# Expert stage of a two-layer hybrid block: padded groups of 32 rows on four 32-column tiles, and a third set of expert weights

## What is computed

```python
def moe(h, w_router, b_router, w1_l, w3_l, w2_l):
    comb = route(hf, w_router, b_router)          # top 2 of 4 experts in the best of 4 groups
    def chunk(args):
        xc, gc = args
        a = jnp.einsum('td,edf->tef', xc, w1_l)   # w1, w3: (16, 1024, 512)
        b = jnp.einsum('td,edf->tef', xc, w3_l)
        u = jax.nn.silu(a) * b * gc[..., None]
        return jnp.einsum('tef,efd->td', u, w2_l) # w2: (16, 512, 1024)
```

## Time and profile before

| what | value |
|---|---|
| median of the three runs | 1327.61 us |
| span of the profiled execution | 1325.8 us, 1.8 us less than the median |
| PE / PEld / DVE / ACT / POOL busy | 82% / 46% / 26% / 16% / 6% |
| bytes over the DMA engines | 328.6 MB, 248 GB/s on average |
| expert stage of layer 0, first up product to last down product | 428.7 to 733.75 us |
| expert stage of layer 1 | 1031.5 to 1296.4 us |
| granted TensorE clock, mean | 0.918 of 2.4 GHz |

### The profile page before, as it was taken

How to read it: one execution, slowest core, us unless ns; L and a number is a source line. 1 busy time by engine, 2 the same in 40 slices (tenths; PEclk the granted TensorE clock), 3 DMA queues, 4 the chain that set the end, 5 groups by cost and what they waited for, 6 DMA issues and landing times.

```text
span 1325.8 us, 18500 instructions
## 1 busy us (share of the span) xinstructions
PE 1081.6 (82%) x6246; PEld 604.7 (46%) x6247; DVE 345.4 (26%) x812; ACT 208.4 (16%) x487; POOL 79.0 (6%) x126
## 2 busy tenths in 40 slices
PE   2799989988981999999899189989892898788771
PEld 1446447765450544444346044647642454344430
DVE  2201147565342100101011430157624011000002
ACT  1110023432010111111101211023300111011001
POOL 2000000001002000000000300000101000000001
PEclk8899999989985999999999689999985799999896
DMA  9923116576135899999369671313645699999993
GB/s 330 374 91 127 64 70 238 202 258 226 43 131 208 319 396 395 398 397 384 122 227 397 214 269 64 127 64 128 240 158 198 234 332 397 396 396 397 397 397 110
DMA packets 142294, 328.60 MB, mean 248 GB/s; under 512 B 6552, under 2 KB 8760, under 8 KB 142240
## 3 DMA queue, kind: packets, MB, share of 16 engines
q1 hardware_dynamic: 125424, 287.84, 58.9%
q0 software_dynamic: 7856, 25.61, 5.4%
q10 hardware_dynamic: 8960, 14.40, 3.1%
HBM read 308.10 MB, written 19.73 MB: 247 GB/s over the span
## 4 chain that ended last, share of the span: by engine, by line
PE 56%; DMA 29%; DVE 7%; ACT 3%; issue 3%; POOL 2%; SPq 0%; ACTq 0%; DVEq 0%; POOLq 0%
DMA ring<-in_w 23%; PE S L1217 17%; PE S L1398 10%; PE S L1327 6%; PE O L1281 4%; PE T L1155 3%; PE AUX L1172 3%; DMA ring<-in_w_ada 3%; PE S L1432 2%; PE T L1432 2%; PE S L1248 2%; PE S L1402 2%; ACT R L643 1%; PE S L1437 1%; DVE R L916 1%
## 5 line engine op out<-in xcount | busy, mean ns | idle before, releaser
L1217 PE MATMUL S<-ring,hT 128*128 128x512 f32 (+1 forms) x576 | 226.0, 548 | 2.3 <-ACT hT L587 2.3
L1402 PE MATMUL S<-ring,R 128*64 128x256 f32 x1472 | 181.1, 405 | 33.0 <-DMA ring<-in_w 28.3
L1402 PEld LDWEIGHTS S<-ring,R 128*64 128x64 f32 x1472 | 114.5, 146 | 106.3 <-DMA ring<-in_w 40.3
L1217 PEld LDWEIGHTS S<-ring,hT 128*128 128x128 f32 x576 | 108.0, 191 | 104.3 <-issue 98.6
L1398 PE MATMUL S<-ring,R 128*128 128x512 f32 x320 | 144.1, 610 | 6.5 <-issue 3.3
L1155 PE MATMUL T<-cst,R 128*128 128x128 f32 (+1 forms) x497 | 80.1, 292 | 64.2 <-DVE R L793 30.4
L1088 DVE SCALAR_TENSOR_TENSOR R<-R,S 128x256 f32<-128x256 f32 (+1 forms) x33 | 16.6, 502 | 412.7 <-ACT R L694 412.7
L1155 PEld LDWEIGHTS T<-cst,R 128*128 128x128 f32 (+1 forms) x497 | 60.2, 151 | 93.4 <-DVE R L793 30.7
L1398 PEld LDWEIGHTS S<-ring,R 128*128 128x128 f32 x320 | 62.1, 195 | 87.2 <-issue 82.4
L1437 PE MATMUL S<-ring,R 128*64 128x512 f32 x368 | 84.0, 598 | 9.6 <-DMA ring<-in_w 5.7
L1327 PE MATMUL S<-ring,hT 128*128 128x512 f32 x192 | 85.6, 607 | 2.3 <-issue 2.3
(11 more groups left out here) (143 smaller groups left out, 756.8 us busy)
## 6 DMA issues: line engine op xcount, KB each, us to landing
ring<-in_w SPq DMA_DIRECT2D x96, 2048.0 KB, 11.5
ring<-in_w_ada SPq DMA_DIRECT2D x24, 2048.0 KB, 8.1
ring<-in_w_in SPq DMA_DIRECT2D x8, 2048.0 KB, 10.8
R<-x_d POOLq DMA_DIRECT2D x45, 256.0 KB, 5.7
ring<-in_w_out SPq DMA_DIRECT2D x4, 2048.0 KB, 9.8
R<-mod_d SPq DMA_DIRECT2D x12, 512.0 KB, 9.6
y_d<-R ACTq DMA_DIRECT2D x46, 128.0 KB, 5.3
y_d<-R ACTq DMA_DIRECT2D x20, 256.0 KB, 6.5
```

What stands on the lines that cost most here:

```text
L1217: ins = pe.matmul(S[:, i % 4, 0:width], hT[:, k, t * P:(t + 1) * P], w[:, k, :], start=(k == 0), stop=(k == KC - 1))
L1402: ins = pe.matmul(S[64 * h:64 * h + 64, i, 0:256], xT[:, half, k % 4, k // 4, 0:64], part[i][:, k, h * 256:h * 256 + 256], start=(k == 0), ...
```

## The change

Every expert's rows now start at a multiple of 32 rows in x_d and y_d, and an item is always one group of 32 rows. An expert with c rows has max(1, ceil(c/32)) groups. All of x_d, and the part of y_d that no group might write, are zeroed early in layer 0, with 30 DMAs of 128 rows each, 15.7 MB together. On TensorE the stationary operand is 128x32 and the four column tiles take a quarter of the output columns each (128 moving columns in the up products, 256 in the down product). The order in an item is: up with w1, the transposes of the next group's rows, the transpose of the last group's u, up with w3, the down product of the last group. xg, xT, u_s, uT, th, t2 and y_s have one buffer each. ACT issues four stores per item in place of two, and it copies the next y only when the four stores of the last one have landed. POOL fetches group i+1 only when group i has been transposed.

The weights have nine regions in place of six: hT and two parts of R2, which nothing uses in the expert stage, are the third set. SP issues the load of an expert when the expert three before it is done, still with at most two in flight. gF is therefore loaded at the end of the stage, into hT. The weights ka, va and kvb of layer 1's projection are issued ahead of the wait for the end of layer 0's experts. The order of some loads in layer 1's attention changes too, and the counts are ready ahead of the gates' computation in place of behind it.

The diff, cut to its core (inside the loops, waits on counts_ready and register steps are left out without a mark):

```diff
-TILE = 64
-MAXW = TOK // P
+ROWS = 32
+MAXG = TOK // ROWS
+SETS = 3
...
+    n_groups = [TOPK * TOK // ROWS + NE, TOPK * SEQ // ROWS + NE]
+    x_tiles = [-(-(g + 1) * ROWS // P) for g in n_groups]
...
-        xg = R2[:, 0:1536].rearrange("p (b n) -> p b n", b=3)
-        y_s = R2[:, 4096:6144].rearrange("p (b n) -> p b n", b=2)
+        zeros = R3[:, 4096:5120]
+        xg = R3[:, 0:256]
+        xT = R3[:, 256:512].rearrange("p (h j t) -> p h j t", h=4, j=2)
+        u_s, uT, th, t2 = R3[:, 512:640], R3[:, 640:768], R3[:, 768:896], R3[:, 896:1024]
+        y_s = R2[:, 9376:9632]
...
         def load_expert(l, e, part):
-            load(("e", l, e, part), 3 * (e % 2) + part, expert_src(l, e, part))
+            slot = 3 * (e % SETS) + part
+            load(("e", l, e, part), slot, expert_src(l, e, part))
+            last[slot] = (s["w2_free" if part == 2 else "w13_free", l], e + 1)
+
+        def spare_free(l):
+            n = sum(len(qtiles[m]) for m in range(l + 1))
+            return [(s["wout_done"], 2 * n), (s["wout_out"], 2 * n), (s["h_ready"], 2 * n)]
...
+        for i in (6, 7, 8):
+            last[i] = spare_free(0)[i - 6]
+        for e in range(2, NE):
+            for part in range(3):
+                load_expert(0, e, part)
+        loads.append("gf0")
+        for u, slot in zip(UNITS[:3], (3, 4, 5)):
+            load_in(1, u, slot)
+        loads.append("drain0")
...
+        spare = [hT[:, :, :].rearrange("p k n -> p (k n)"), R2[:, 0:SLOTCOLS], R2[:, SLOTCOLS:2 * SLOTCOLS]]
+        slots = [ring[:, i, :] for i in range(6)] + spare
...
+                    pool.wait_ge(s["zeros_made"], 1)
+                    pool.wait_ge(s["proj_done"], 1)
                     for m in range(DEPTH):
+                        for b in range(x_tiles[m]):
+                            pool.dma_start(x_d[m][b * P:(b + 1) * P, :], zeros).then_inc(s["tail_zeroed"], 16)
+                        for b in range(NE * ROWS // P):
+                            r = (n_groups[m] - NE) * ROWS + b * P
+                            pool.dma_start(y_d[m][r:r + P, :], zeros).then_inc(s["tail_zeroed"], 16)
...
+                fetch(0)
+                with pool.Fori(0, n) as i:
                     pool.wait_ge(s["counts_ready"], l + 1)
+                    pool.wait_ge(s["rows_flipped", l], r_flips)
+                    fetch(i + 1)
...
+                def store(item):
+                    for j in range(4):
+                        act.dma_start(y_d[l][ds(ROWS * item, ROWS), 256 * j:256 * j + 256],
+                                      y_s[32 * j:32 * j + 32, :]).then_inc(s["y_stored", l], 16)
...
+                with act.Fori(2, n) as i:
+                    act.wait_ge(s["up1_done", l], r_next)
+                    gate_up()
+                    act.wait_ge(s["up3_done", l], r_next)
+                    take_rows()
+                    act.wait_ge(s["down_done", l], r_done)
+                    act.wait_ge(s["y_stored", l], r_stored)
+                    copy(y_s, y_bank).then_inc(s["y_out", l], 1)
+                    act.wait_ge(s["y_out", l], r_next)
+                    store(i - 1)
...
+                def up(bank, w, up_done):
+                    for k in range(KC):
+                        for q in range(4):
+                            ins = pe.matmul(bank[32 * q:32 * q + 32, :], xT[:, k // 2, k % 2, :], w[:, k, P * q:P * q + P],
+                                            start=(k == 0), stop=(k == KC - 1))
+                    ins.then_inc(s[up_done, l], 1)
...
+                def down(w, first=False):
+                    for q in range(4):
+                        for j in range(4):
+                            ins = pe.matmul(y_bank[32 * j:32 * j + 32, :], uT[:, 32 * q:32 * q + 32], w[:, q, 256 * j:256 * j + 256],
+                                            start=(q == 0), stop=(q == 3))
+                    ins.then_inc(s["down_done", l], 1)
...
+                def item(e, first, rep):
+                    pe.wait_ge(s["rows_taken", l], r_next)
+                    pe.wait_ge(s["t2_done", l], r_done)
+                    up(a_bank, own[0], "up1_done")
+                    pe.wait_ge(s["rows_in", l], r_have)
+                    flip_rows(first)
+                    pe.wait_ge(s["u_done", l], r_done)
+                    flip_up()
+                    up(b_bank, own[1], "up3_done")
+                    pe.wait_ge(s["u_taken", l], r_done)
+                    pe.wait_ge(s["y_out", l], r_done)
+                    down(prev[2], first)
```

More of the change, by code:

```diff
@@ L562, in square_sum @@
                 squares[0] += 1
-                act.activation(junk, X[:, t, :], ACT.Square, accum_out=ssq[:, c0 + c:c0 + c + 1]).then_inc(s["act_ssq"], 1)
-            n_items, n_more = act.alloc_register("act_items"), act.alloc_register("act_more")
-            act.reg_mov(n_items, 0)
-            act.reg_mov(n_more, 0)
-            tiles = act.alloc_register("act_tiles")
-            wide, narrow, next_first, before, down = (act.alloc_register(f"act_{n}")
-                                                      for n in ("wide", "own_wide", "next_first", "before", "down"))
+                act.activation(out, X[:, t, :], ACT.Square, accum_out=ssq[:, c0 + c:c0 + c + 1]).then_inc(s["act_ssq"], 1)
+            r_done, r_next, r_stored = (act.alloc_register(f"act_{n}") for n in ("done", "next", "stored"))
             for l in range(DEPTH):
@@ L743, in _ @@
+                act.wait_ge(s["counts_ready"], l + 1)
+                act.wait_ge(s["down_done", l], r_done)
+                act.wait_ge(s["y_stored", l], r_stored)
+                copy(y_s, y_bank).then_inc(s["y_out", l], 1)
+                act.wait_ge(s["y_out", l], r_next)
+                store(n - 1)
                 act.wait_ge(s["counts_ready"], l + 1)
@@ L783, in _ @@
                 ada_out(x)
-            n_items = dve.alloc_register("dve_items")
-            dve.reg_mov(n_items, 0)
-            wide = dve.alloc_register("dve_wide")
+            r_done, r_next = (dve.alloc_register(f"dve_{n}") for n in ("done", "next"))
             for l in range(DEPTH):
@@ L1177, in _ @@
                 ada(x)
-            n_items = pe.alloc_register("pe_items")
-            pe.reg_mov(n_items, 0)
-            n_more, have, emptied, last_y = (pe.alloc_register(f"pe_{n}") for n in ("more", "have", "emptied", "last_y"))
-            pe.reg_mov(n_more, 0)
-            tiles = pe.alloc_register("pe_tiles")
-            wide, own_wide, now = (pe.alloc_register(f"pe_{n}") for n in ("wide", "own_wide", "now"))
+            r_done, r_next, r_have, r_more = (pe.alloc_register(f"pe_{n}") for n in ("done", "next", "have", "more"))
             for l in range(DEPTH):
@@ L1193, in _ @@
                 for k in range(KC):
-                    transposes(("hT", l, k), [xn[:, t, k * P:(k + 1) * P] for t in range(TT)])
+                    transposes(("hT", l, k), [xns[l][:, t, k * P:(k + 1) * P] for t in range(TT)])
                 taken(("hT", l, KC - 2))
@@ L1310, in _ @@
                 mixT(qtiles[l][-1])
-                slots = [weights(("out", l, n)) for n in (0, 1)]
+                out_slots = [weights(("out", l, n)) for n in (0, 1)]
                 def out_proj(t):
@@ new lines, in _ @@
+                others(0, slice(0, 1), 0)
+                reps = (NE - 1) // SETS
+                with pe.Fori(0, reps) as rep:
+                    for e in range(1, SETS + 1):
+                        item(e, True, rep)
+                        others(e, ds(SETS * rep + e, 1), rep)
+                for e in range(1 + SETS * reps, NE):
+                    item(e, True, 0)
+                    others(e, slice(e, e + 1), 0)
+                pe.wait_ge(s["counts_ready"], l + 1)
+                pe.wait_ge(s["u_done", l], r_done)
```

499 lines of the change are left out of this document (187 added, 312 removed).

## The result

Four runs of the changed kernel gave 1391.94 to 1409.52 us, median 1398.82, beside 1325.61 (1322.47 to 1328.58) for the kernel before in the same session. The ratio is 1.056, 95% interval 1.051 to 1.062. The forecast was 1313 us with a range up to 1350, so it missed by 86 us and on the wrong side. The profiled execution took 1395.1 us, with a span of 1393.4.

The account below looks back on a forecast made before the run. Layer 0's expert stage was taken as bound by TensorE, layer 1's by weight loads. 1325.8 - 8.4 (layer 0) - 6 (layer 1) = 1311.4, plus 1.8 around the span, gave 1313 us, range 1278 to 1350.

Parts of the forecast that it names:

- TensorE's work in an item: TensorE, expert stages: up and down products, transposes and shape changes of one 32-row item sum to 5.9 us.
- (a): Store loop on ACT: copy y, issue four stores, wait for landing before the next copy; 7.5 us loaded, 4.5 quiet.
- (b): Fetch loop: transposes, POOL's issue, then landing of the next group's rows; 6.4 us loaded, 3.9 quiet.
- (c): ACT's order: next item's tanh stands behind the stores, and the down product waits for it; 6.5 us, loaded or not.
- Four tiles load beside their products: TensorE's up and down products: weight loads overlap the running products, so an up group of four takes 109 ns.
- rival 3: Four tiles' weight loads don't overlap their products: item 10.3 us, setting the period, total 1430 us; chance 0.08.
- Period 7.3 us: Layer 0's time per item: 0.8 of the loaded store loop's 7.5 us plus 0.2 of ACT's order's 6.5 us.
- Layer 0, start at 433.7: Layer 0's first item starts 5 us later than 428.7, as third-set loads share the DMA engines with POOL's scatters.
- Layer 0, net -8.4: Layer 0's stage: last down product at 721.5, 12.2 us earlier; last store 7.5 us behind it, not 3.75; net 8.4 saved.
- Layer 1, net -6: Layer 1's stage: last weight landing 16 us earlier, tail behind it 10 us longer, for 6 us saved.
- Zeroing at nothing: Layer 0's first projection: 30 zeroing DMAs (15.7 MB, 40 us) hide under it and cost nothing.
- Rival 4: The kernel doesn't do what it says: loops take more or fewer groups than 64; any side, chance 0.03.

Follow-up runs that it names:

- one copy: The changed kernel with a single copy of the item's TensorE code per expert, a branch picking the down product, and w1/w3 freed at the expert's end: 1296.3 us.
- few loads: Weight loads of experts 3 to 15 left out in both layers (output differs): 1259.2 us from the changed kernel, 1180.8 us from one copy.
- experiments 4 and 2: 4: one copy with its three-expert loop opened into fifteen experts, 1319.5 us. 2: the kernel before with its loop over expert pairs opened four times, 1372.6 us.

## Why the prediction was wrong

The step that failed is the term that the sum did not have. It was "TensorE's work in an item": so many records by 27 or 55 ns, as if the code that issues them cost nothing. The item holds 160 matmul records where the narrow item holds 80, and there are two copies of it for each of three experts in one loop. Nothing in the rows of before would have priced this, since its loop stayed at hand: 37 packets in the whole span. But the list of queues did show code as traffic, and the sum doubled the instructions of an item without asking where they come from. In my own terms it was a fourth loop beside (a), (b) and (c), put at nothing without a reason. It cost 102 us (1398.8 against 1296.3): 56 in layer 0's stage, 42 in layer 1's.

Point by point:

- **TensorE's work, 5.9 us.** Right: 27 ns a record up, 1.91 us down, and 5.84 us between down products when nothing waits.
- **Four tiles load beside their products** (so not rival 3). Right: a group of four takes 109 ns, the weight loads beside it. The time of 1399 lies near rival 3's 1430, by another mechanism; its own sign, a group over 150 ns, is absent wherever the clock was up.
- **Period 7.3 us.** Right where code was at hand: 282.8 us for 39 items are 7.25 in one copy. Its parts were a little long: (a) and (b) together hold 7.2, (c) is 6.2 in place of 6.5 (its terms as listed add up to 6.6; the narrow item, from its rows, is 11.9 us and not 11.8). The quiet store was taken at 1.8 us and landed in 1.5; the loaded one was taken at 4.8 and the loaded fetch at 5.3:

```profile
R<-x_d POOLq DMA_DIRECT2D x66, 128.0 KB, 5.6
y_d<-R ACTq DMA_DIRECT2D x256, 32.0 KB, 4.9
```

- **Layer 0, start at 433.7.** The changed kernel started at 431.8, one copy at 428.7, as before the change. That looks as if the third set's loads had cost the scatters 0 to 3 us in place of 5. They cost more, and other parts of the change hid it: the scatters began at 405.0 and 402.2 in place of 407.5. From the last scatter to the first fetch POOL waited 13.1 us in the changed kernel, 12.8 in one copy and 4.5 in the kernel before; without a third set, 5.4. So the collision was worth some 8 us. One copy, then two sets in the changed kernel:

```profile
424.99 0.62 POOL L472 DMA_DIRECT2D R<-x_d  x1 [12.78 <-issue]
```

```profile
417.24 0.62 POOL L466 DMA_DIRECT2D R<-x_d  x1 [5.42 <-issue]
```

- **Layer 0, net -8.4.** Measured with the code at hand: last down product at 711.6, 22 earlier than before; the forecast had 721.5. In the changed kernel: 771.1.
- **Layer 1, net -6.** The forecast was 260.7 us from the first up product to the last store's landing (1033.5 to 1294.2), in place of 268.7; measured with the code at hand: 254.2 (1014.2 to 1268.4), so -14.5. The bound (weight loads at 391 GB/s; 396 were moved from 1080 to 1240) and the clock were right: up products of 3.64 us in place of 1.95, at 1.2 GHz (granted 0.50), after the pauses of 7.5 us. Of the 6.5 us, 1.2 are in the last load's landing (242.3 us after the first up product, forecast 243.5) and 5.3 in the tail behind it: 11.9 us in place of 17.2, since expert 15's second item had begun (1254.5) before that load landed (1256.5) and ran at 1.95 us an up product.
- **Zeroing at nothing.** Right: the projection's steps are as before, and the first one is even 3 us earlier (48.47 in place of 51.74).
- **Rival 4**, it doesn't do what it says: no, 64 items were done (8192 up records at 128 each).

The signs of being wrong listed in the forecast were a period, a slow group of four and a wait for the zeroing; the one that came up, TensorE idle in the middle of a product with no releaser, was not among them. With this step put right, the others give 1296 us, within the range's lower half: an error of 17 us from small terms, and of 102 us from the missing one. That the period came out right (7.25 for 7.3) with each of its loops a little long is in part luck.

**What stays open**: how much of one stall is the jump and how much the wait for the block behind it (no run held one fixed and moved the other), and where between 1,360 and 2,020 instructions a loop stops staying at hand.

## What to carry to other kernels

Count the instructions of a loop body as you count its bytes. Splitting a product into more, smaller ones and giving each weight set and each special case its own copy both multiply code, and on TensorE code that must come in again on each pass has a price: 98 of the 630 us of the two stages here beside full DMA queues, and 81 of 494 with few loads. Look at the instruction queue's packets, and at idle time put down to issue that falls inside a product. "Issue" alone does not prove it: with two sets most of it was a wait for weights with a register load behind it, and what told them apart was whether a packet of code came in the gap. Then fix it in the code (one copy with a branch) before judging the idea: here the same idea went from 5.6% slower to 2.3% faster, and with two buffers and one reordered instruction to 5.1% faster than the kernel before.

## What the runs showed of the hardware that I had not expected

- A loop of some 1,230 instructions on TensorE fetched nothing on its later passes (7 packets a stage, all in its first 54 us), nor did one of some 1,360; one of some 2,020 fetched about all of itself on each of five passes (46 and 50 packets). The Trainium skill, "Runtime: NRT & Kernel Launch", Instruction fetch mechanics, gives TensorE room for 2,048 instructions. The loops of 1,230 and 1,360 agree with that; the one of some 2,020 would just fit by it and did not stay. The same section says further on that only two blocks are held, which these runs don't bear out, since the five or so blocks of each of these two loops stayed. It also calls the refill mostly hidden and says that kernels prefer full unrolling where possible; here unrolling cost 23 and 44 us (experiments 4 and 2).
- Blocks of code came 6 to 7 us apart while the weights' loads ran and 4 to 5 us apart without them, though one packet took only about 1 us.
- Four column tiles of 32, each with its own fp32 weights of 32 columns, take 109 ns a group, the loads included.
- A 32 KB store landed in 1.5 us on quiet engines and in 4.9 beside the weight loads.
